# A two-layer decoder trunk in split float32: another begin, router stage and end

## The reference

```
layer 0: x += retention(norm(x))        # 4 heads, w_in (1024, 6144), w_out (2048, 1024)
         x += (silu(h Wg) * (h Wu)) Wd  # h = norm(x), width 2816
shared:  k, v = split(norm(x) @ w_kv), rotary on k
layer 1: x += diff_attention(norm(x), k, v)   # 8 heads, two softmaxes each,
                                              # heads normed, then @ w_o (1024, 1024)
         h = norm(x); logits = h @ w_router   # (256, 8)
         gates = softmax over the two largest logits of a token, 0 elsewhere
         for e in range(8):                   # width 3584
             x += (silu(h Wg[e]) * (h Wu[e])) Wd[e] * gates[:, e]
out = norm(x) * final_gain
```

## Time and profile before

| | us |
|---|---|
| median of 3 runs (lowest, highest) | 1523.16 (1522.74, 1523.5) |
| profiled execution | 1523.38 |
| its span, first to last instruction | 1521.5 |

### The profile page before, as it was taken

The page is one execution under the profiler, slowest core; times in us unless marked ns, Lnnn a source line. Parts: engine busy times, 40 slices in busy tenths (PEclk is TensorE's granted clock), DMA queues, the critical chain, the costliest instruction groups (busy, mean ns, idle before and its releaser), DMA issues.

```text
span 1521.5 us, 18733 instructions
## 1 busy us (share of the span) xinstructions
PE 1484.6 (98%) x6858; PEld 1228.9 (81%) x6858; DVE 1173.2 (77%) x922; ACT 972.1 (64%) x829; POOL 43.0 (3%) x43
## 2 busy tenths in 40 slices
PE   7999999999999889999999999999999999999996
PEld 6878788888788778888888888888888888888885
DVE  6464455555686568888888888888888888888896
ACT  4544453444447557777777777777777777777774
POOL 1000000000000000000000000000000000000000
PEclk9999999999999989999999999999999999999999
DMA  9644445554453149999999999999999999999992
GB/s 384 274 169 146 178 166 195 192 194 149 156 198 135 65 164 373 371 376 387 374 378 385 381 371 394 369 381 382 378 380 377 372 381 377 383 367 379 424 383 84
DMA packets 64876, 455.31 MB, mean 299 GB/s; under 512 B 7200, under 2 KB 7328, under 8 KB 11456
## 3 DMA queue, kind: packets, MB, share of 16 engines
q1 hardware_dynamic: 61344, 440.92, 75.9%
q0 software_dynamic: 3488, 13.80, 2.3%
HBM read 446.82 MB, written 7.86 MB: 299 GB/s over the span
## 4 chain that ended last, share of the span: by engine, by line
PE 92%; DVE 4%; ACT 2%; issue 2%; DMA 0%; DVEq 0%; SPq 0%; POOLq 0%; POOL 0%; ACTq 0%
PE psum L1488 29%; PE psum L1490 28%; PE psum L1489 28%; PE psum L1521 3%; DVE w_lo L1027 2%; ACT w_hi L720 1%; PE psum L1641 0%; PE psum L1542 0%; PE psum L1772 0%; PE psum L1729 0%; DVE x_sb L1062 0%; PE psum L1714 0%; PE psum L1534 0%; DMA x_sb<-in_x 0%; DVE x_sb L1423 0%
## 5 line engine op out<-in xcount | busy, mean ns | idle before, releaser
L1027 DVE TENSOR_TENSOR w_lo<-raw,w_hi 128x2048 fp32r<-128x2048 f32 (+1 forms) x420 | 948.6, 2274 | 237.9 <-ACT w_hi L720 237.8
L720 ACT CAST w_hi<-raw 128x2048 fp32r<-128x2048 f32 (+1 forms) x420 | 799.5, 1904 | 318.9 <-PE psum L1490 317.2
L1488 PE MATMUL psum<-w_hi,actA_hi 128*128 128x512 f32 (+1 forms) x1376 | 542.5, 394 | 5.1 <-DVE w_lo L1027 2.6
L1490 PE MATMUL psum<-w_hi,actA_lo 128*128 128x512 f32 (+1 forms) x1376 | 534.2, 388 | 0.0
L1489 PE MATMUL psum<-w_lo,actA_hi 128*128 128x512 f32 (+1 forms) x1376 | 533.5, 388 | 0.0
L1488 PEld LDWEIGHTS psum<-w_hi,actA_hi 128*128 128x128 f32 x1376 | 259.2, 188 | 58.2 <-DVE w_lo L1027 4.5
L1490 PEld LDWEIGHTS psum<-w_hi,actA_lo 128*128 128x128 f32 x1376 | 259.1, 188 | 54.0
L1489 PEld LDWEIGHTS psum<-w_lo,actA_hi 128*128 128x128 f32 x1376 | 259.5, 189 | 50.7 <-issue 0.5
L1488 PE MATMUL psum<-w_hi,actB_hi 128*128 128x512 f32 x632 | 247.9, 392 | 4.9 <-DVE actB_lo L1398 1.5
L1490 PE MATMUL psum<-w_hi,actB_lo 128*128 128x512 f32 x632 | 246.1, 389 | 0.0
L1489 PE MATMUL psum<-w_lo,actB_hi 128*128 128x512 f32 x632 | 245.9, 389 | 0.0
(11 more groups left out here) (161 smaller groups left out, 474.8 us busy)
## 6 DMA issues: line engine op xcount, KB each, us to landing
raw<-in_moe_w_gate SPq DMA_DIRECT2D x112, 1024.0 KB, 7.1
raw<-in_moe_w_up SPq DMA_DIRECT2D x112, 1024.0 KB, 7.4
raw<-in_moe_w_down SPq DMA_DIRECT2D x112, 1024.0 KB, 7.1
raw<-in_ret_w_in SPq DMA_DIRECT2D x22, 1024.0 KB, 12.5
raw<-in_ffn_w_gate SPq DMA_DIRECT2D x11, 1024.0 KB, 4.7
raw<-in_ffn_w_up SPq DMA_DIRECT2D x11, 1024.0 KB, 4.9
raw<-in_ffn_w_down SPq DMA_DIRECT2D x10, 1024.0 KB, 4.8
raw<-in_ret_w_out SPq DMA_DIRECT2D x8, 1024.0 KB, 4.8
```

The costliest lines, as they stand in the source:

```text
L720: nc.scalar.copy(w_hi[:, u % SPLIT_SLOTS, 0:size], raw[:, u % RAW_SLOTS, 0:size]).then_inc(sem["hi_ready"], 1)
L1027: nc.vector.tensor_tensor(w_lo[:, slot, 0:size], raw[:, u % RAW_SLOTS, 0:size], as_f32(w_hi[:, slot, 0:size]), ALU.subtract).then_inc(sem[ ...
L1488: nc.tensor.matmul(dst, l_hi[:, k, cols], r_hi[:, kk, rcols], start=first, stop=False)
L1490: return nc.tensor.matmul(dst, l_lo[:, k, cols], r_hi[:, kk, rcols], start=False, stop=last)
```

## The change

- **Begin.** The first constants are asked for by ScalarE's queue, no longer ahead of x in SP's. ScalarE makes a tiny activation as soon as they are there. The chunks of the norm go through six banks instead of four and in pairs, with a weight unit behind each pair. TensorE makes 14 idle transposes of the identity before the first chunk and 4 behind each pair.
- **Attention.** The squares of the first four heads are summed one and one softmax later; the statistics are kept and raised to -1/2 by tile; the projection's first unit waits for each tile's remainder alone.
- **Router.** VectorE takes one weight remainder fewer ahead of the last two sums into x. The last projection unit is cut up: half of tile 0, turning of the chunks 0 to 3, the rest of tile 0, three quarters of tile 1, `route(0)`, the last quarter. The gate tables are made in 10 small instructions (w1, w2, gate, second_gate, e_gates, e_rows, e_route), ahead of the split of the gathered rows. GpSimd scales `h_rows` instead of ScalarE.
- **Last expert.** In every item the two last down units hold one half of the columns each (the host lays the weights out so). In the last item the seventh turn stands between the two down units before it, with buffers of its own; `y_back` is added one step earlier; `combine` starts on the columns 0.
- **End.** VectorE multiplies the first half of a row by the gain while the power is taken, ScalarE scales that half, VectorE does the other.

```diff
@@ order of TensorE's results
+    router_turn(range(4))
     o.group(("wo", 1, 0))
-    router_turn(range(4))
+    both(("router",), C0, "router_read", 0)
     o.unit(("wo", 1, 1))
-    both(("router",), C0, "router_read", 0)
...
+            for half in range(2):
+                if last and s == STEPS - 1 and half:
+                    e_turn(at, STEPS)
+                o.unit(*([(at, "e_down", half)] if s == STEPS else []))
@@ sync
-            sp.dma_start(const[:, 0:CONST_FIRST], table[:, 0:CONST_FIRST]).then_inc(sem["ident_in"], 16)
@@ gpsimd
+            for half in range(2):
+                for t in (1, 0):
+                    root(f"sub{half}t{t}")
             root("ffn1")
+            pool.wait_ge(sem["pe_done"], w.pe("gather", 1))
+            for t in range(TILES):
+                nc.gpsimd.tensor_scalar(h_rows[:, t, :], h_rows[:, t, :], rstd("ffn1", t), None, ALU.mult
+                                        ).then_inc(sem["hn_scaled"], 1)
@@ scalar
+            act.dma_start(const[:, 0:CONST_FIRST], table[:, 0:CONST_FIRST]).then_inc(sem["ident_in"], 16)
             act.wait_ge(sem["ident_in"], 16)
-            norm_hi(0, actA_hi, range(4))
-            hi_through(1)
-            norm_hi(0, actA_hi, range(4, KC))
-            hi_through(AHEAD)
+            nc.scalar.activation(lam[:, 6:8], c_("ident", 0, 2), ACT.Copy, scale=gain_col(0, 0)).then_inc(sem["table_in"], 1)
+            for n in range(FIRST_UNITS):
+                norm_hi(0, actA_hi, range(2 * n, 2 * n + 2))
+                if n < AHEAD:
+                    hi_through(n + 1)
+                if n == AHEAD - 1:
+                    hi_through(SPLIT_SLOTS)
...
-                if i == 4:
+                if i == 5:
                     o_squares(0, (1,))
-                if i == 5:
+                if i == 6:
                     o_squares(0, (0,))
...
             router_x(range(4))
             used += 1
-            hi_through(used + AHEAD)
             square_sums("ffn1", (0,))
...
+            for t in range(TILES):
+                act.wait_ge(sem["gained"], t + 1)
+                act.wait_ge(sem["rstd"], RSTD.index("final") + t + 1)
+                nc.scalar.activation(out_rows[:, t, 0:BLK], out_rows[:, t, 0:BLK], ACT.Copy, scale=rstd("final", t)
+                                     ).then_inc(sem["scaled"], 1)
@@ vector
+            used += 2
+            lo_through(used + AHEAD - 1)
+            add_to_x(("wo", 1, 0), 0, 1, 31)
             rows_times_gain(0)
-            used += 2
-            lo_through(used + AHEAD)
+            rows_times_gain(1, (0,))
             for t in range(TILES):
-                add_to_x(("wo", 1, t), t, 1, 30 + t + 1)
+                nc.vector.tensor_scalar(e_tokens[:, t, :], c_("iota", 0, 2 * N_EXPERTS), 0.0, c_("token", t, 1), ALU.mult, ALU.add)
+            add_to_x(("wo", 1, 1), 1, 1, 32)
...
-            lo_through(used + SPLIT_SLOTS)
+            lo_through(used + AHEAD)
+            dve.wait_ge(sem["gap_exp"], 1)
...
             gathered(("gather",), 0)
...
+            lo_through(used + SPLIT_SLOTS)
+            choose(0, 0)
+            rest_of_current(0)
...
-                    if last and 3 <= s <= 6:
-                        k, t = divmod(s - 3, 2)
+                    if last and 2 <= s <= 5:
+                        k, t = divmod(s - 2, 2)
@@ tensor
+            def idle(n):
+                for _ in range(n):
+                    nc.tensor.transpose(bank(("ret", 0, 0))[:, 0:P], c_("ident"), c_("ident"))
+
             pe.wait_ge(sem["ident_in"], 16)
-            turn_norm(0, range(KC))
+            idle(14)
+            for c in range(0, KC, 2):
+                turn_norm(0, range(c, c + 2))
+                idle(4)
...
-            pe.wait_ge(sem["o_lo"], 2)
-            project(("wo", 0), A, BLK, KC, 2, u1=1)
+            for t in range(TILES):
+                pe.wait_ge(sem["o_lo"], t + 1)
+                project(("wo", 0), A, BLK, KC, 2, u1=1, tiles=(t,))
...
-            project(("wo", 1), A, BLK, KC, 2, u0=1, tiles=(0,))
+            project(("wo", 1), A, BLK, KC, 2, u0=1, tiles=(0,), part=(0, 1))
             turn_norm(4, range(4))
-            project(("wo", 1), A, BLK, KC, 2, u0=1, tiles=(1,))
-            pe.wait_ge(sem["x_sum"], 31)
+            project(("wo", 1), A, BLK, KC, 2, u0=1, tiles=(0,), part=(2, 3))
+            project(("wo", 1), A, BLK, KC, 2, u0=1, tiles=(1,), part=(0, 1, 2))
+            pe.wait_ge(sem["small_in"], 16)
+            route(0)
+            project(("wo", 1), A, BLK, KC, 2, u0=1, tiles=(1,), part=(3,))
             for t in range(TILES):
-                if t:
-                    pe.wait_ge(sem["small_in"], 16)
-                    route(0)
-                    pe.wait_ge(sem["x_sum"], 32)
+                pe.wait_ge(sem["x_sum"], 31 + t)
```

More of the change, by code:

```diff
@@ L379, in item @@
                 hidden((at, "e_gate", s), G0, ("e_sil", s + 1))
-            o.open((at, "e_turn", s - 1), T0, ("e_turn_lo", s), known_free=True)
-            o.group((at, "e_turn", s - 1))
+            if not (last and s == STEPS):
+                e_turn(at, s)
             if s == 5 and not last:
@@ L997, in item @@
                     used += 2
-                    hi_through(min(used + AHEAD, limit))
+                    hi_through(min(used + AHEAD, limit - 1 if last and s == STEPS - 1 else limit))
                 for c in range(2):
@@ L1354, in combined, with each, twice @@
                     nc.vector.tensor_tensor(v, v, bank((*key, q)), ALU.add).then_inc(sem["comb"], 1)
-            lo_through(used + SPLIT_SLOTS)
+            lo_through(used + AHEAD)
+            dve.wait_ge(sem["gap_exp"], 1)
+            step(nc.vector.tensor_scalar(w2, gap_e, 1.0, None, ALU.add))
+            step(nc.vector.reciprocal(w1, w2))
+            step(nc.vector.tensor_tensor(w2, w1, gap_e, ALU.mult))
+            def each(column):
+                return column.rearrange("p (t o) -> p t o", o=1).to_broadcast([P, TILES, N_EXPERTS])
+            def twice(v):
+                return v.rearrange("p t (o e) -> p t o e", o=1).to_broadcast([P, TILES, 2, N_EXPERTS])
+            step(nc.vector.tensor_tensor(gate, first, each(w1), ALU.mult))
+            step(nc.vector.tensor_tensor(second_gate, second, each(w2), ALU.mult))
+            nc.vector.tensor_tensor(e_gates.rearrange("p t (o e) -> p t o e", o=2), twice(gate), twice(second_gate), ALU.add)
+            for t in range(TILES):
+                nc.vector.tensor_scalar(e_rows[:, t, :].rearrange("p (o e) -> p o e", o=2), wide(second[:, t, :], 2), c_("y_row", t, 1), None, ALU.add)
+            for half in range(2):
+                step(nc.vector.tensor_scalar(e_route[:, 0:2, half * N_EXPERTS:(half + 1) * N_EXPERTS], place, -float(P * half), None, ALU.add))
             gathered(("gather",), 0)
@@ L1497, in _, with project @@
             done = order.unit_done
-            def project(key, left, n, kc, units, u0=0, u1=None, tiles=range(TILES), norm=None):
+            def project(key, left, n, kc, units, u0=0, u1=None, tiles=range(TILES), norm=None, part=None):
                 per = kc // units
@@ L1506, in project @@
                             ready((*key, t))
-                        for kk in range(per):
+                        for kk in part or range(per):
                             k = u * per + kk
@@ L1777, in _ @@
             eT = (chunks(eT_hi, P), chunks(eT_lo, P))
+            eT_end = tuple(chunks(v, P) for v in eT_last)
             every = slice(0, P)
@@ L1821, in _, with turn_hidden @@
             loop_start = list(count)
+            def turn_hidden(at, s):
+                pe.wait_ge(sem["e_hid"], w.at("e_hid", s))
+                turn((at, "e_turn", s - 1), e_hid, 4)
             def item(at, last):
@@ L1827, in item @@
                         hidden((at, "e_gate", s), units)
-                    pe.wait_ge(sem["e_hid"], w.at("e_hid", s))
-                    turn((at, "e_turn", s - 1), e_hid, 4)
+                    if not (last and s == STEPS):
+                        turn_hidden(at, s)
                     if s == 5 and not last:
```

129 lines of the change are left out of this document (58 added, 71 removed).

## The result

| us | before | after |
|---|---|---|
| median (lowest to highest, 4 runs each) | 1523.22 (1522.74 to 1523.5) | 1509.63 (1507.78 to 1510.52) |
| profiled execution | 1523.38 | 1510.07 |
| its span | 1521.5 | 1508.2 |

The ratio is 0.9904, 95% interval [0.9892, 0.9916]: 13.6 us faster in the medians, 13.3 in the two profiled executions, where the forecast was 16.8.

A forecast was written before the change was run, and what follows sets the result against it. TensorE was taken as the bound, busy 1484.6 of 1521.5 us; only begin, attention's end with router, and end could give. 4.2 + 1.4 + 7.7 + 3.7 - 0.2 = 16.8, so 1506.4 us against the median; range 1502.5 to 1513.

The forecast's parts named there:

- 1. Begin: Start of the kernel: earlier, warm first product near 10.1 us; gain 4.2 us, ends 4.8 and -0.5.
- rival A: Begin and router: the clock doesn't follow, begin gives about -0.5, router loses about 2 more; 1513.0 us, chance 15%.
- land 2.0 us after issue, about 2.8 as before: Begin: constants asked for by ScalarE's queue arrive as early as before, so idle transposes start at 2.8 us.
- They cost nothing because x is not there before: Begin: the 14 idle transposes, 3.1 us until 5.9, are free because x has not landed yet.
- 2. Attention: Last softmaxes and first output projection: squares moved, statistics split, projection starts on tile 0 alone; gain 1.4 us (0.3 to 2.0).
- 3. Router: Last projection unit through M4's product: earlier sums, MAX8, gather and first expert product; gain 7.7 us (5.5 to 8.6).
- Rival C: GpSimd's row scaling costs what its power costs, 420 us, delaying the first fetch; about 1840 us, chance 3%.
- rival B: Router to first expert: VectorE becomes the bound between 540 and 560 us; 3 to 4 us lost, 1510 us, chance 12%.
- the prediction's worry: Router: GpSimd's scaling and two-input VectorE instructions block each other, putting M3's remainder 0 to 1.5 us behind TensorE.
- 4. End: Last item and output: wait before last down unit goes, combining and norm start earlier; gain 3.7 us (3.0 to 4.2).
- The y_back sums: Last item: four sums moved one step (17 us) earlier, no wait, one no longer hidden; -0.2 us.
- Rival D: Expert loop: bound by DMA (0.98) and takes the gain back; no change, 1522 us, chance 2%.

The follow-up runs named there:

- again: The kernel after, run once more unchanged: 1509.12 us, ratio 0.9907 to before.
- old_begin: The kernel after with the whole begin of the kernel before put back, everything else as after: 1510.91 us, ratio 0.9907 to before.
- no_idle: The kernel after without any idle transposes: 1507.81 us, ratio 0.9900 to before; its repeat took 1507.94 us, ratio 0.9893.
- two_ahead: The kernel after with VectorE taking unit M1's weight remainder ahead of the last two sums into x again: 1513.21 us, ratio 0.9925 to before.
- warm_router: The kernel after with 19 idle transposes in the router's two waits and the gate tables behind the gathered rows' split: 1511.02 us, ratio 0.9914 to before.
- no_idle_sp: The kernel after without idle transposes and with the constants first in SP's queue again: 1508.56 us, ratio 0.9889 to before.
- ident_sp: The kernel after with the first constants asked for by SP ahead of x again: 1508.53 us, ratio 0.9899 to before.

## Why the prediction was right, and where it was off

**Forecast and range.** 1506.4 was forecast and 1509.63 measured, inside 1502.5 to 1513. The sign, the router and the loop are as forecast; the begin and the end were sized too high, and the attention's gain was there but paid back at the low clock in this profile.

**1. Begin: sized 4.2, measured 2.3 to 2.6 (3.3 in `again`).** The warm first product came true, and with it rival A fell for this stage. It came at 12.03 instead of 10.1, though. The step that failed is "land 2.0 us after issue, about 2.8 as before": from ScalarE's queue, issued at the same moment as SP's first large transfer, they took 3.9 us, so TensorE's 14 idle transposes ran from 4.70 to 7.74. "They cost nothing because x is not there before" fell with it. The prediction named this risk in half a sentence (a late queue would eat into the idle transposes) and then gave it no price. The second failure is deeper: that these transposes are needed. All three profiles without them were warm from the first product, and the two with the constants by ScalarE's queue reached 4.0 and 4.3. Against old_begin, cold until 17.6, they differ in that the norm is turned in one stretch, and in the banks and the early activation. The Trainium skill (TensorE: Matmul & The Clock Gate, Part 1) has it that the throttled clock is the default and activity releases it; the trace agrees: sixteen transposes, fifteen of them from 6.15 to 9.36, were followed by products 0.23 us apart.
Two slips in the sum cancel out. Fourteen idle transposes until 5.9 and 32 more with a rise at 8.5 end at 10.5 by the prediction's own 0.22 and 0.10, not 10.1; and 17.2 with cast and remainder make 21.4, not 21.2. The 21.4 is what the gain was taken from, and it held (21.53 and 21.12 in no_idle and its repeat), so the 4.2 is right for a begin without the transposes that were to bring it.

**2. Attention: sized 1.4, measured 1.68 (old_begin: 1.98 with 0.34 of it from an earlier first product), then -1.6 in the profile.** Two of its steps held: from the pair's turn to the next one 0.8 us went (forecast 0.7), and from the heads' turn to the first product 0.8 (0.7). Between them, one didn't. The second power was to lie beside the attention's matmuls, which ended at 505.4. They ended there because they ran at the low clock (granted 0.50 from 503 to 505, 2.77 us for the last twelve); in after these twelve took 1.57 us, and TensorE then waited 1.13 us for VectorE, and VectorE 1.12 for GpSimd's powers. The stretch is 3.0 us long both times, so the 1.68 is in part luck. And the term had no price for the clock of the projection: the first product followed a wait of 1.79 us before and 0.97 now, and yet the low clock now falls on it in half of the profiles. Rival A spoke of the begin and of the router only. The kernel before had a low stretch in this stage too, on those last matmuls.

**3. Router: sized 7.7, measured 7.8.** The steps held one by one, read on the times of before (after plus 2.65): MAX8 537.56 against 537.3, gather 541.1 against 540.5, first expert product 546.4 against 546.2, M4 557.7 against 557.8. The tables ahead of xe_lo cost nothing, because at 542.91 VectorE waited for ScalarE. The gather itself was not warm (5.49 us), and the range of that step had it (by the prediction's own numbers a cold gather ends at 546.2; its 547.4 is the first product behind it).
That this profile hit the number is partly luck as well. Step by step the forecast needs a warm second half of the router's product. It was warm in after, where the low clock began at 535.2 and lasted 6.8 us, and cold in old_begin and two_ahead, where it began at 532.9 and lasted some 13.7 us, as long as in before. With the same router's edits old_begin has 35.09 us from the second heads' turn to the first expert product, against 32.35 in after and 37.66 before: there rival A came true for the router, at 2.7 us, a little over the 2 that it was given. What decides when the clock falls stays open.
GpSimd's scaling took 3.3 us a tile, outside the 1 to 2 us taken and far from the other end; it ended at 550.69, and the first fetch is at 637.52, so it was free. Rival C is out by it, rival B did not come to bear: the remainder beside the scaling took 2.28 us, as everywhere. What was blocked were two instructions with one SBUF input of data, by 0.66 us in all. The Trainium skill (SBUF — State Buffer, Who interferes with whom) has it that a VectorE instruction with two SBUF inputs contends with a GpSimd one that reads SBUF, by an exclusive lock; the trace agrees at the end of the kernel (power 0.95 us beside such a product, 0.57 alone) but here the remainder, with two SBUF inputs, kept its 2.28 us, and by the measurement the prediction's worry did not come true. How much of GpSimd's 3.3 us is waiting for VectorE no run tells, since the scaling never ran alone; in warm_router, with VectorE's work in another order beside it, it took 2.9.

**4. End: sized 3.5 with the -0.2, measured 2.9.** No wait is left ahead of the last down unit. Less the 10.43 us that the end comes earlier, the sums were due at 1500.87 and over at 1501.14, tile 0 due out at 1502.87 and issued at 1503.33. 0.3 of the difference is there before the norm; in the norm the power, which was taken at its duration of before (0.57 us), took 0.38 longer for each tile, and not all of it shows. The y_back sums, priced at 0.2, are taken up next.

**Loop and last item.** The prediction put nothing on the loop, and the sum up to the last item's sixth turn is nothing, but of two parts. An item is 119.0 us long in before (647.97 to 1361.95 are six of them; 118 was the length of the stretch in the table, not of an item) and 118.93 in after, so that the lead of 10.43 us at the first hidden block had grown to 10.89 at the last item's first one (1404.19 before, 1393.30 after). In the last item 0.45 was given back at once: VectorE's first y_back sum, one step earlier now (1418.58, 1.22 us), stands ahead of three weight remainders, and TensorE waited for one of them until 1422.06. From there on the lead is 10.4 again (1489.91 and 1479.48). So by the timeline the y_back sums did cost about 0.45 us, at their new place and not at the end (no run leaves them out), and that the loop gave as much is luck; why its items are shorter stays open. Rival D is out.

## What to carry to other kernels

Before adding filler work to warm an engine, run the kernel without it, with the needed work in one stretch; filler that starts late stands in front of the first product. A DMA moved to another queue has another landing time even if it is issued at the same moment, so price the move by what else is in flight then. An earlier first product is worth only as much as the next transfer that the stage waits for allows. Where two executions of one kernel differ by the size of a term, compare the same events in several profiles before crediting an edit.

## What the runs showed of the hardware

- 92 KB of constants landed 2.0 us after issue when they were first in SP's queue, and after 3.9 to 4.2 us when ScalarE's queue issued them beside SP's first 512 KB of x. The first weight unit (512 KB) was then asked for at 1.66 instead of 2.13 us and landed at 7.1 to 7.8, against 8.0, 8.8 and 8.9 in no_idle_sp, ident_sp and old_begin; in the kernel before, constants first in SP's queue too, it was 7.5.
- The place where TensorE falls to the 1.2 GHz level is not fixed by the program: the same kernel had it at the projection (0.54 from 504.2 to 507.9) in one execution and not in the next, for 1.6 us. TensorE was busy all through 534 to 543 in warm_router and was still granted 0.62. In the router the level was low for 13.7 us in before, old_begin and two_ahead, 6.8 in after, and 3.5 in no_idle and its repeat.
- A power of one column on GpSimd took 0.57 us alone and 0.95 beside a VectorE product of 128 x 512 with two SBUF inputs; a multiply of 128 x 1024 by a column took 3.3 us on GpSimd beside VectorE's work (2.9 in warm_router), 1.1 on ScalarE.
- The profile's clock column reads 1.00 in the begin (14 to 16 us in before), where products stand 0.43 us apart, as they do at a granted 0.50 elsewhere.
